# Two modulation groups summed on VectorE, the sink taken into the score maximum, and gates evicted at other units

## The reference, cut to what matters

```python
m = jnp.max(s, axis=-1, keepdims=True)
if sink is not None:
    m = jnp.maximum(m, sink)
e = jnp.where(mask, jnp.exp(s - m), 0.0)
den = jnp.sum(e, axis=-1, keepdims=True)
if sink is not None:
    den = den + jnp.exp(sink - m)
```

## Time and profile before

| | |
|---|---|
| median of 3 runs | 884.95 us (884.6 to 885.35) |
| time of the profiled execution | 884.18 us |
| its span in the trace | 882.4 us |
| granted clock, mean | 0.996 |

### The profile page before, as it was taken

How to read it: one execution, slowest core, us unless ns; L and a number is a source line. 1 busy time by engine, 2 the same in 40 slices (tenths; PEclk the granted TensorE clock), 3 DMA queues, 4 the chain that set the end, 5 groups by cost and what they waited for, 6 DMA issues and landing times.

```text
span 882.4 us, 17028 instructions
## 1 busy us (share of the span) xinstructions
PE 863.6 (98%) x6944; PEld 817.8 (93%) x6944; DVE 408.9 (46%) x1015; ACT 468.2 (53%) x706; POOL 674.2 (76%) x552
## 2 busy tenths in 40 slices
PE   7999999999989999999999999999999999999997
PEld 6899899998879999889997899999999999999997
DVE  3899745635785576953554223321124642210001
ACT  4545766377876623344444565875336665534431
POOL 0987549748935799798767787678899899987880
PEclk9999999999999999999999999999999999999998
DMA  8855586884210597876575444545546555545521
GB/s 324 339 186 198 204 292 226 307 313 144 87 59 2 205 408 261 344 276 242 195 268 181 166 144 148 188 143 192 191 147 246 191 186 188 189 144 191 192 96 48
DMA packets 28484, 177.62 MB, mean 201 GB/s; under 512 B 3144, under 2 KB 5844, under 8 KB 8056
## 3 DMA queue, kind: packets, MB, share of 16 engines
q1 hardware_dynamic: 27112, 174.87, 54.0%
q10 hardware_dynamic: 1296, 1.68, 0.6%
HBM read 174.95 MB, written 3.43 MB: 202 GB/s over the span
## 4 chain that ended last, share of the span: by engine, by line
PE 95%; DVE 2%; ACT 1%; issue 1%; POOL 1%; DMA 1%; POOLq 0%; SPq 0%; DVEq 0%; ACTq 0%
PE proj L793 20%; PE proj L795 19%; PE proj L796 19%; PE proj L829 4%; PE proj L874 3%; PE proj L872 3%; PE proj L875 3%; PE mixed L1021 1%; PE scores L976 1%; PE transposed L990 1%; PE proj L1074 1%; PE proj L1143 1%; PE mixed L1004 1%; PE scores L963 1%; PE proj L1077 1%; PE proj L1076 1%
## 5 line engine op out<-in xcount | busy, mean ns | idle before, releaser
L695 POOL TENSOR_TENSOR w_lo<-raw,w_hi 128x512 fp32r<-128x512 f32 x348 | 445.2, 1320 | 126.3 <-ACT w_hi L1434 126.3
L795 PE MATMUL proj<-parts,w_lo 128*128 128x256 f32 x1000 | 279.4, 279 | 0.6 <-POOL w_lo L695 0.6
L793 PE MATMUL proj<-parts,w_hi 128*128 128x256 f32 x952 | 270.3, 284 | 0.6 <-POOL w_lo L695 0.4
L796 PE MATMUL proj<-parts,w_hi 128*128 128x256 f32 x952 | 265.8, 279 | 0.0
L1434 ACT ACTIVATE w_hi<-raw 128x2048 fp32r<-128x2048 f32 x84 | 161.0, 1917 | 109.3 <-DMA raw<-in_weights 58.9
L795 PEld LDWEIGHTS proj<-parts,w_lo 128*128 128x128 f32 x1000 | 188.1, 188 | 1.7 <-POOL w_lo L695 0.8
L793 PEld LDWEIGHTS proj<-parts,w_hi 128*128 128x128 f32 x952 | 179.0, 188 | 3.4 <-issue 2.2
L796 PEld LDWEIGHTS proj<-parts,w_hi 128*128 128x128 f32 x952 | 179.0, 188 | 0.0
L695 POOL TENSOR_TENSOR w_lo<-arena,w_hi 128x512 fp32r<-128x512 f32 (+2 forms) x56 | 67.7, 1245 | 27.3 <-ACT w_hi L1434 27.3
L1446 ACT ACTIVATE arena<-proj 128x512 f32<-128x512 f32 x32 | 18.9, 597 | 53.2 <-PE proj L796 36.5
L872 PE MATMUL proj<-w_hi,parts 128*128 128x512 f32 x112 | 45.1, 403 | 0.0
(11 more groups left out here) (448 smaller groups left out, 2157.0 us busy)
## 6 DMA issues: line engine op xcount, KB each, us to landing
raw<-in_weights SPq DMA_DIRECT2D x106, 1024.0 KB, 5.0
arena<-in_weights SPq DMA_DIRECT2D x31, 1024.0 KB, 7.6
wide<-in_weights SPq DMA_DIRECT2D x9, 1024.0 KB, 6.9
probT<-in_weights SPq DMA_DIRECT2D x8, 1024.0 KB, 5.0
dil_lines<-dil_line SPq DMA_DIRECT2D x1, 2304.0 KB, 12.3
prob<-in_weights SPq DMA_DIRECT2D x2, 1024.0 KB, 4.8
dil_bias<-dil_lines SPq DMA_DIRECT2D x1, 1536.0 KB, 9.8
xT<-in_x SPq DMA_DIRECT2D x4, 256.0 KB, 5.6
```

The costliest lines, as they stand in the source:

```text
L695: nc.gpsimd.tensor_tensor(lo_slots[RAW_AT[n]][:, at], raw_slots[RAW_AT[n]][:, at], hi_slots[HI_AT[m]][:, at].bitcast(F32), ALU.subtract).t ...
L793: nc.tensor.matmul(dst, whi, h, start=first, stop=False)
L795: nc.tensor.matmul(dst, wlo, h, start=False, stop=False)
L796: last = nc.tensor.matmul(dst, whi, lo[:, k, :], start=False, stop=stop)
```

## The change

- Groups 0 and 1 leave TensorE: `ada` and `ada_out` go, `ADA_FIRST` has eight loads in place of four, and `first_half` runs eight times in place of four. The first one stands ahead of `variance("kskw")`; the last one stands ahead of `variance("cmp")` without its flip, which follows behind `head_norm_end("kd")`. Since `po` then holds the sums, the norms cmp and kd use `pt`.
- The loads of `ADA_FIRST` go ahead of `ck0, qd0, cv1, qd1, kd, zc0, zd0, zd1`. Ring slots and banks are dealt out anew without `ad0` and `ad1`.
- In part b `za1` is projected in two halves, the second one at unit 3, directly ahead of `B:wo0`.
- In parts c and d the gates `zc0`, `zc1`, `zd1` are evicted at units 1, 4 and 12 (before: 0, 3 and 13), and one scaling of a bias moves from behind unit 2 to behind unit 3.
- In part d the sink is the start value of the score maximum. `exps` takes `exp(sink - max)` in four instructions of one column each.

```diff
-FILL_B = [x.split() for x in ("zb1.0 S: zb1.1 ad0 L:mean E:zb0", "za0 L:sq E:zb1 E:ad0 L:centre", "za1 E:za0 L:var", "ad1 B:wo0 L:scale")]
+FILL_B = [x.split() for x in ("zb1.0 S: zb1.1 L:mean E:zb0", "za0 L:sq E:zb1 L:centre", "za1.0 E:za0 L:var", "za1.1 B:wo0 L:scale")]
 FILL_CD = [x.split() for x in (
-    "S: N:kd E:zc0", "zc1.0 E:kd", "zc1.1", "E:zc1", "modA zd0.0.0", "zd0.0.1 E:modA", "",
-    "zd0.1", "zd1.0 E:zd0", "", "zd1.1.0", "zd1.1.1", "L:y0", "H:0 E:zd1 L:y1", "H:1", "")]
-SCALE_BEFORE, SCALE_BEHIND = {6: (0, 1), 12: (1, 1)}, {2: (0, 0), 7: (1, 0)}
+    "S: N:kd", "zc1.0 E:zc0 E:kd", "zc1.1", "", "E:zc1 modA zd0.0.0", "zd0.0.1 E:modA", "",
+    "zd0.1", "zd1.0 E:zd0", "", "zd1.1.0", "zd1.1.1", "E:zd1 L:y0", "H:0 L:y1", "H:1", "")]
+SCALE_BEFORE, SCALE_BEHIND = {6: (0, 1), 12: (1, 1)}, {3: (0, 0), 7: (1, 0)}
-ADA_FIRST = ("ad2a", "ad2b", "ad3a", "ad3b")
+ADA_FIRST = tuple(f"ad{g}{x}" for g in range(4) for x in "ab")
-FIRST_BEFORE = ("ck0", "qd0", "cv1", "qd1")
-FIRST_AFTER = ("wo0_3", "kskw", "qc0", "qc1")
+FIRST_BEFORE = ("ck0", "qd0", "cv1", "qd1", "kd", "zc0", "zd0", "zd1")
+FIRST_AFTER = ("wo0_3", "kskw", "qc0", "qc1", "vdgt", "hidk", "qd0", "hidv")
...
-                if part == "d":
-                    last = nc.scalar.activation(s[:, 12:16], s[:, 12:16], ACT.Exp)
+                for i in range(4) if part == "d" else ():
+                    last = nc.scalar.activation(s[:, 12 + i:13 + i], sink_of(at, i), ACT.Exp, bias=s[:, 4 + i:5 + i])
...
-                own.did(V.reciprocal(po[:, 0:w], rstd[:, 0:w]))
+                own.did(V.reciprocal(pt[:, 0:w], rstd[:, 0:w]))
...
-                                                     scale=q_rstd[:, "bcd".index(part), at, i8:i8 + 1], scalar=-3e38,
+                                                     scale=q_rstd[:, "bcd".index(part), at, i8:i8 + 1],
+                                                     scalar=sink_of(at, i) if part == "d" else -3e38,
...
-                sk, down = (cut(v[:], 4)[:, :, 2 * at:2 * at + 2] for v in (sinks, no_sinks))
-                own.did(V.tensor_tensor(cut(top, 2), cut(top, 2), down, ALU.min))
-                own.settle()
-                own.did(V.tensor_copy(s[:, 4:8], top))
-                V.tensor_tensor(cut(s[:, 12:16], 2), cut(top, 2), sk, ALU.add).then_inc(mx_ready, 1)
...
-            ada_out("ad1")
...
+            first_half(0)
             variance("kskw")
             head_norm_end("kskw", "kskw", None, None)
-            first_half(0)
+            first_half(1)
...
-            first_half(1)
+            first_half(2)
             for name in ("qc0", "qc1"):
                 variance(name)
                 head_norm_end(name, name, None, None)
-                first_half(2 + int(name[2]))
+                first_half(3 + int(name[2]))
+            first_half(5)
             variance("qd0")
+            first_half(6)
+            half_rows(ADA_FIRST, 7, silu_c, po, sem("first_used"))
             variance("cmp")
...
             head_norm_end("kd", "kd", None, None)
+            first_columns(7)
             score_max(PART["c"][1])
```

## The result

| | before | after |
|---|---|---|
| median | 884.95 us (883.76 to 886.38, 7 runs) | 890.43 us (887.09 to 892.48, 7 runs) |
| ratio, 95% interval | | 1.0054 (1.0045 to 1.0064) |
| profiled execution, span | 884.18, 882.4 us | 887.99, 886.0 us |
| granted clock, means of the runs | 0.995 to 0.998 (99 runs beside the experiments) | 0.991 to 0.993 |

The change makes the kernel 0.54% slower. The forecast was 884.7 with a range up to 886.9; the result lies 5.7 us above the forecast and outside of the range.

The account below looks back on a forecast made before the run. The prediction took TensorE's work, 95% of the chain, plus its gaps to bound the kernel. Its terms, -3.70 + 1.88 + 1.7 - 0.15 = -0.3 us, took the median from 884.95 to 884.7 us, range 882.3 to 886.9.

Parts of the forecast that it names:

- Part b: Ahead of `wo0`: removed products save 3.70 us, operand waits give back 1.88 (first wait some 1.6), 1.82 are left.
- The loads and the halves: VectorE, 155 to 200 us: halves 4 to 7 wait for loads; half 7 runs 198.7 to 201.9, `variance("cmp")` follows at 202.1.
- everything lies 1.8 us earlier: Loads of halves 4 to 7, on the clock of before: the shift changes nothing, since TensorE gates the other loads.
- The fit that the prediction takes from the Trainium skill: Load times: a DMA takes 2.0 us plus bytes / 436 GB/s, an estimated 4.4 us for a lone unit.
- The size of the stall at the compressed norm: TensorE's sums of qd1, due at 200.47, wait for `variance("cmp")`: 1.7 us idle, bounds nothing to 6 us.
- The stretch at 188: Between part b and the compressed norm: everything taken as 1.8 us earlier, with no term for a wait here.
- Parts c and d: Moved gates and the sink in the score maximum: -0.15 us together, bounds -1.2 and +0.8.
- Second output projection: Load of `ak2_0` issued later, ACT's split starts 2.4 us later; costed at nothing, some 3 us of cover left.
- The sum: Whole kernel: -3.70 + 1.88 + 1.7 - 0.15 = -0.3 us, median 884.7 us, no change that can be measured.
- the slower one: Load queue in the second layer's projections: 3.47 us a unit, half 7 ends at 206.8, stall 6.3 us, 889.3; chance 0.12.

Follow-up runs that it names:

- the run with short loads: The changed kernel with the loads of `ad3a` and `ad3b` cut to an eighth of their bytes, group 3 not computed: 885.24 us, ratio 1.0001.
- all but the gates: The changed kernel with `FILL_CD` (the gates' places in parts c and d) and the bias scalings of before: 888.39 us, ratio 1.0037.
- A pure wait of 2.0 us: The kernel before with six idle VectorE transposes ahead of the instruction of `variance("cmp")`, no added loads or half sums: 889.71 us, ratio 1.0061.
- TensorE kept busy through it: The kernel before with six idle VectorE transposes ahead of `variance("cmp")` and 16 more overwritten products at the head of kd's bank: 887.41 us, ratio 1.0025.
- the early loads: The changed kernel with the loads of `ad3a` and `ad3b` ahead of `zc1` and `zd0`, in place of `zd0` and `zd1`: 886.04 us, ratio 1.0016.
- group 0 alone: The kernel before with only group 0 moved to VectorE; `ad1` stays on TensorE, gates and sink as before: 883.24 us, ratio 0.9985.
- TensorE kept busy through the stall: The changed kernel with the gates and scalings of before and 25 more overwritten products at the head of kd's bank: 887.50 us, ratio 1.0031.
- the kernel with `zc1` at unit 3: The kernel before with `zc0` evicted at unit 1 and `zd1` at 12, `zc1` and the bias scaling as before: 884.34 us, ratio 0.9991.
- the kernel with products ahead of `wo0`: The changed kernel with `ad3a` and `ad3b` loaded earlier, gates of before, and 13 more products ahead of the first of `wo0_0`: 886.76 us, ratio 1.0012.
- the 5 products that cover the wait: The kernel before with group 0 moved to VectorE, `ad1` on TensorE, and 5 more overwritten products ahead of `kc2`: 882.87 us, ratio 0.9976.
- the moved gates alone: The kernel before with the changed kernel's gate evictions and bias scaling; groups 0 and 1 on TensorE, sink as before: 886.78 us, ratio 1.0025.
- the first group: The kernel before, run again beside the first four experiments (23 runs): 884.61 us.

## Why the prediction was wrong, step by step

**Part b: right.** The products are gone, the wait for the first piece is 1.5 us (forecast 1.6), that for the second 0.2. At the landmark of rows 3, the 60 products of `wo0`, which start at 118.56 in place of 119.71, 1.15 are won, and 1.93 if the later start-up is taken off; 1.82 were forecast. The clock stayed at 1.00 there, so this wait cost its own length and no more.

**The loads and the halves: the chain right, its place wrong.** Halves 4 to 7 wait for their loads as forecast, and `variance("cmp")` behind them. The numbers look right too, 198.42 for half 7 where 198.7 was forecast, and 201.68 for `variance("cmp")` where it was 202.1, but they are on different clocks. The forecast is on the clock of before, with the remark that "everything lies 1.8 us earlier" changes nothing. TensorE reached this stretch 1.15 us earlier than before (1.93 won, 0.78 of later start-up), and the last halves didn't: on the clock of the forecast, half 7 stands at 198.42 + 1.15 = 199.57, 0.9 late. The queue was full (425 GB/s from 191 to 197, and the 389 of rows 8 in the forecast), so the halves followed the loads and not TensorE. That the queue was faster than forecast hid a part of it, which is luck. The fit that the prediction takes from the Trainium skill, "DMA: Bandwidth & Descriptors", section on the anatomy of one DMA, is given there for DMAs that GpSimd issues, and these loads are SP's.

**The size of the stall at the compressed norm: wrong, the step that failed.** The prediction's term is "TensorE idles 1.7 us", and the last two loads cost 5.2 (the run with short loads). Two things were missing. The wait itself is longer: by the place of the halves it would be 202.02 - 199.3 = 2.7 us, of which the fall of the clock at 191 took up 1.6, so that 1.07 is seen; where no fall stands ahead of it, 3.0 is measured (all but the gates). And the prediction took a wait for its length. A pure wait of 2.0 us at that place costs 4.7, and 2.5 with TensorE kept busy through it. The column that shows it, the granted clock, stands in rows 2 at 1.00, and the prediction read it there without asking what would keep it at 1.00.

**The stretch at 188: missed.** The prediction held that part b's gain passes through to 200. At 188 TensorE has only small products, and ScalarE is due there just ahead of it. In the profiled execution TensorE comes 1.3 us earlier and ScalarE 1.2, and TensorE now waits for it, 0.17 us in the changed kernel, 0.44 with the early loads, 0.46 with group 0 alone, 0.86 in the trace of TensorE kept busy through the stall; the clock then fell to half in each of the four. It costs 1.7 us in the profiled execution. The wait doesn't do it each time: with 0.23 us in the kernel with `zc1` at unit 3 the clock stayed at 1.00, and so it did with the 0.35 us of the kernel with products ahead of `wo0`, whose rows there are

```profile
196.00:198.00 2.00, 1.65 (x15) 1.56 (x15) 1.93 (x5) 1.54 (x5) 1.91 (x3) 1.00 1.02 430
198.00:200.00 2.00, 2.00 (x19) 2.00 (x19) 1.97 (x6) 1.88 (x9) 0.00 (x0) 1.00 1.02 422
```

With the same small products and no wait it stayed at 1.00 in every trace (the changed kernel with the gates of before, among others). That, and the 5 products that cover the wait, speak for the wait as part of the cause; what decides when it does is open.

The Trainium skill, "TensorE: Matmul & The Clock Gate", section on the second failure mode (psum-queue depth-cycling), says that frequent short idle times between groups of matmuls can make the clock swing between its two levels. Here single waits of 0.17 to 4.7 us were enough for a fall in some executions. The same page of the Trainium skill, section on oscillation, prices the half clock at half of the time spent in it. The losses above are worked out in the same way, and the landmark at c1 agrees: 3.33 by the sum, 3.17 measured.

**Parts c and d: wrong in sign, the second step that failed.** Forecast -0.15, measured +2.2 for the moved gates alone. It is the sentence "With `zc1` evicted at unit 4, ... the transposes of c6 come out at today's time". The prediction worked out where VectorE's multiply lands, and not what ScalarE has to do before the tanh:

```profile
227.54 0.60 ACT L1530 ACTIVATE probT<-proj 128x512 f32<-128x512 f32 x1 [2.43 <-PE mixed L1025]
228.04 0.59 ACT L1530 ACTIVATE probT<-transposed 128x512 f32<-128x512 f32 x1
228.51 1.27 ACT L1514 ACTIVATE dil_bias<-arena,q_rms 128x128 f32<-128x128 f32 x4
229.69 0.59 ACT L1540 ACTIVATE arena<-proj 128x512 f32<-128x512 f32 x1
```

```profile
231.05 0.39 PE L1076 MATMUL proj<-parts,w_hi 128*128 128x256 f32 x1 [1.53 <-DVE arena L2054]
```

The tanh of `zc1` (line 1540) now stands behind `transposed_out` of unit 3 (line 1530), which waits 2.43 us for the mix of c2, and behind the scaling that moved there too (line 1514). `zd0` wants the bank that this gate frees, and TensorE waits 1.5 us for it. The prediction saw just this chain for `zc0` ("`zc1` needs the bank that this gate frees") and did not follow it for the next gate. `zc1` at unit 3 and the other moves kept gave -0.7, where -0.15 was forecast for all moves together; the interval (0 to -1.6) holds both.

**Second output projection: right.** No wait for a split of `ak2_0` is in the list.

**The sum, with the measured terms**, on the 884.6 of the first group: -3.7 + 1.9 (part b) + 5.2 (last two loads, with both falls of the clock) + 2.2 (gates, with theirs) = 890.2, and 890.43 is measured. Since the 5.2 is itself the changed kernel less the one with short loads, what this tests is the rest: -3.7 + 1.9 + 2.2 gives 885.0 for short loads, and 885.24 is measured. Of the rivals, the slower one gave 889.3 by a stall of 6.3 us from a slow queue. It came close in number by luck and was wrong in mechanism: the queue was faster than the forecast's, and in the trace more time went into the clock (3.4 us) than into the waits at 190 and at the norm (1.2).

## What to carry to other kernels

A wait of the engine that bounds a kernel isn't worth its length only. When an edit takes work off TensorE ahead of a place where another engine or a load is due just in time, price the idle time and then the half clock that may follow it, and read the granted clock of each run before reading the waits. Work that fills such a wait was free here (`ad1`), and taking it away won nothing. A full load queue doesn't move with the engine that got faster, so a forecast on the clock of before has to say for each engine and queue whether it comes earlier too. And when an eviction moves, follow it through the queue of every engine in it, up to who wants the bank.

## What the runs showed of the hardware

A wait of 2.0 us took 4.7 us. The granted clock of TensorE fell from 2.4 to 1.2 GHz at the earliest within the wait (the execution with 3.0 us, from 199.4 to 202.4: 0.78 in the window from 201 to 202, and 0.50 from 202 to 211), and in the changed kernel 2.8 us behind its end (202.02; the window from 204 to 205 has 0.92). It did not fall each time: the 1.5 us wait for `zc1`'s bank was followed by 0.67 and 0.50 in one trace and by 1.00 in three others, and the 1.5 us wait at `wo0` by 1.00 in all of them. That makes the runs scatter: the runs of one kernel with a mean clock of 0.997 or 0.998 lie within 2.4 us of each other, and a kernel whose clock falls spreads over 5 and more (887.09 to 892.48 for the changed one).

One VectorE instruction of 128x512, which took 0.95 us at the same place in the changed kernel's trace, took 7.14 us in the profiled execution of the kernel with products ahead of `wo0`, and TensorE waited 4.7 us for it. What held it, the trace doesn't show:

```profile
82.12 7.14 DVE L2029 TENSOR_TENSOR prob<-prob,stat 128x512 f32<-128x512 f32 x1
```
